# Eight products of the output projection moved between the last head steps of a hybrid decoder layer

## What is computed

```python
a_out = mla_prompt(q_nope, q_rope, c_kv, k_r, w_ukv[l])
b_out = combine_dilations([dilated_prompt(qb, kb, vb, wdw, dl) for wdw, dl in DIL_PATTERNS], xp.dtype)
c_out = conv_module(g_ext, conv_w[l], conv_b[l], conv_ln_g[l], conv_ln_b[l])
xp = xp + jnp.concatenate([a_out, b_out, c_out], axis=-1) @ w_out[l]
hf = rmsnorm(xp, norm_ffn[l])
xp = xp + peer_blocked(hf.reshape(B * T, D), peer_wq[l], peer_subkeys[l], peer_u[l], peer_v[l]).reshape(B, T, D)
```

## Time and profile before

| | us |
|---|---|
| median of 3 runs | 2072.3 (2066.62 to 2073.37) |
| profiled execution, time | 2078.74 |
| profiled execution, span | 2076.9 |
| PE busy | 2055.7 (99%) |
| DVE busy | 1530.8 (74%) |
| ACT busy | 1284.6 (62%) |
| mean granted clock of PE | 0.995 |

### The profile page before, as it was taken

One profiled execution on the slowest core, in us unless ns is written; L12 is line 12 of the kernel. 1 busy time (PEld: TensorE's weight loads), 2 busy tenths in 40 slices (PEclk: granted clock), 3 DMA queues, 4 the chain that ended last, 5 costly groups with the idle time before them and its releaser, 6 DMA issues.

```text
span 2076.9 us, 40622 instructions
## 1 busy us (share of the span) xinstructions
PE 2055.7 (99%) x15546; PEld 1794.8 (86%) x15546; DVE 1530.8 (74%) x3491; ACT 1284.6 (62%) x2535; POOL 119.9 (6%) x138
## 2 busy tenths in 40 slices
PE   8999999999999999999999999999999999999998
PEld 6776799999999888788887758999999998887887
DVE  5844589868899776576678436998688997766766
ACT  5464445658888665565564544556688886555654
POOL 2200010000000010100022000100000001101000
PEclk9999999999999999999999999999999999999999
DMA  9443437776666888898763543577766668888886
GB/s 313 154 150 143 163 126 254 248 253 221 216 215 214 286 304 296 303 319 279 253 226 141 170 170 116 180 253 250 246 221 209 220 214 300 311 290 295 266 269 220
DMA packets 137376, 481.76 MB, mean 232 GB/s; under 512 B 25666, under 2 KB 42082, under 8 KB 130768
## 3 DMA queue, kind: packets, MB, share of 16 engines
q1 hardware_dynamic: 124640, 438.45, 62.6%
q0 software_dynamic: 10496, 40.42, 5.6%
q10 hardware_dynamic: 2048, 0.30, 0.1%
HBM read 475.83 MB, written 104.21 MB: 279 GB/s over the span
## 4 chain that ended last, share of the span: by engine, by line
PE 98%; DVE 1%; ACT 1%; DMA 0%; issue 0%; DVEq 0%; ACTq 0%
PE ps L1194 35%; PE ps L1241 33%; PE ps L827 4%; PE ps L875 4%; PE ps L919 3%; PE ps L1206 3%; PE ps L1157 2%; PE ps L927 2%; PE ps L1165 1%; PE ps L1161 1%; PE ps L884 1%; PE ps L1016 1%; PE ps L1180 1%; PE ps L1019 1%; PE ps L978 1%; PE ps L1032 1%
## 5 line engine op out<-in xcount | busy, mean ns | idle before, releaser
L2165 DVE TENSOR_TENSOR parts<-region,parts 128x1024 fp32r<-128x1024 f32 x512 | 625.6, 1222 | 300.6 <-ACT parts L1509 298.0
L1194 PE MATMUL ps<-tokens_hi,parts 128*128 128x256 f32 x4096 | 760.5, 284 | 0.0
L1509 ACT CAST parts<-region 128x1024 fp32r<-128x1024 f32 x512 | 538.8, 1052 | 271.0 <-PE ps L1241 221.2
L1241 PE MATMUL ps<-parts,parts_hw 128*128 128x512 f32 x3024 | 688.7, 389 | 0.0
L1241 PEld LDWEIGHTS ps<-parts,parts_hw 128*128 128x128 f32 x3024 | 566.8, 188 | 124.0 <-DVE parts_hw L2215 6.9
L1194 PEld LDWEIGHTS ps<-tokens_hi,parts 128*128 128x128 f32 x4096 | 636.6, 188 | 1.0 <-issue 0.8
L1194 PE MATMUL ps<-parts_hw,parts 128*128 128x256 f32 x2048 | 573.7, 280 | 0.0
L1194 PEld LDWEIGHTS ps<-parts_hw,parts 128*128 128x128 f32 x2048 | 386.5, 189 | 0.0
L1555 ACT ACTIVATE big<-ps 128x256 f32<-128x256 f32 (+31 forms) x252 | 131.7, 523 | 146.9 <-PE ps L1194 146.8
L1543 ACT CAST parts_hw<-big 128x256 fp32r<-128x256 f32 x256 | 170.9, 668 | 0.7 <-DVE big L2226 0.7
L1536 ACT ACTIVATE region<-region 128x128 f16<-128x128 f16 x512 | 169.2, 436 | 0.0
(11 more groups left out here) (316 smaller groups left out, 2172.9 us busy)
## 6 DMA issues: line engine op xcount, KB each, us to landing
region<-in_peer_uT SPq DMA_DIRECT2D x256, 512.0 KB, 4.1
region<-in_peer_v SPq DMA_DIRECT2D x256, 512.0 KB, 4.7
out<-in_state_win_k SPq DMA_DIRECT2D x112, 384.0 KB
out<-in_state_win_v SPq DMA_DIRECT2D x112, 384.0 KB
big<-in_window_keysT SPq DMA_DIRECT2D x16, 576.0 KB, 3.8
big<-in_state_win_v SPq DMA_DIRECT2D x48, 192.0 KB, 4.2
region<-in_w_out SPq DMA_DIRECT2D x4, 2048.0 KB, 8.2
big<-in_peer_wq SPq DMA_DIRECT2D x4, 2048.0 KB, 13.7
```

The costliest lines, as they stand in the source:

```text
L1194: mm = pe.matmul(ps[:, j % ZB, 0:SEQ], a, hp[b][:, c, :], start=(c == 0 and n == 0), stop=(c == KD - 1 and n == 2))
L1241: mm = pe.matmul(ps[:, 2 * half + t, :], w_t[a][:, 128 * t:128 * t + 128], v_t[b][:, 512 * half:512 * half + 512], start=(j == 0 and n == ...
L1509: act.copy(hi_t[n % HIGHS], rows_t[n % ROWS]).then_inc(high[l], 1)
L2165: dve.tensor_tensor(lo_t[n % ROWS], rows_t[n % ROWS], hi_t[n % HIGHS], ALU.subtract).then_inc(low[l], 1)
```

## The change

Four of the six "mT" turns, with their copies on ACT, move from behind the loop into step 11, ahead of the window mixes. They hold the heads' outputs of passes 0 to 7. The first two sums, ("xo", 0, 0) and ("xo", 0, 1), are split. Their first four products are made by `begin_out(0)` in step 12 (ahead of owT) and `begin_out(1)` in step 13 (behind olT). The last four are made by `end_out` where the whole sums stood. For that, two jobs "begun" are new, which ACT answers with a nop that moves nothing. The sums stay in their banks meanwhile, so the other jobs from "begun" 0 to "ycT" 1 take turns in the six banks left. From ("xo", 0, 0) on each job has the bank it had.

```diff
         if s == WINDOW_MIX:
+            jobs += [(("mT", g), "A") for g in range(4)]
             jobs += [(("ow", 0), "A"), (("ow", 1), "A")]
         if s == WINDOW_MIX + 1:
-            jobs += [(("owT",), "V"), (("wT",), "V")]
+            jobs += [(("begun", 0), "A"), (("owT",), "V"), (("wT",), "V")]
         if s == WINDOW_MIX + 2:
-            jobs += [(("olT",), "V")]
+            jobs += [(("olT",), "V"), (("begun", 1), "A")]
...
-    jobs += [(("mT", g), "A") for g in range(2 * HP)]
+    jobs += [(("mT", g), "A") for g in range(4, 2 * HP)]
...
-BANK = [LATE.get(name, (n if n < NUM["mT", 0] else n + 6) % 8) for n, (name, _) in enumerate(JOBS)]
+OUT_BANK = (NUM["xo", 0, 0] + 4) % 8
+def bank_of(n, name):
+    if name[0] == "begun":
+        return (OUT_BANK + name[1]) % 8
+    if name in LATE:
+        return LATE[name]
+    if n < NUM["begun", 0]:
+        return n % 8
+    if n >= NUM["xo", 0, 0]:
+        return (n + 4) % 8
+    turn = n - NUM["begun", 0] - 1 - (n > NUM["begun", 1])
+    return (OUT_BANK + 2 + turn % 6) % 8
+BANK = [bank_of(n, name) for n, (name, _) in enumerate(JOBS)]
...
+                def turn_mixed(g):
+                    turn("mT", g, parts=[(oAB[:, t, 128 * g:128 * g + 128], 128, 128, 128 * t) for t in range(2)])
+                def begin_out(t):
+                    wait_moved(pe, "mT", 3)
+                    pe.wait_ge(w_ld[now[0]][5 % 2], 16 * (5 // 2))
+                    o = begin("begun", t)
+                    for k in range(4):
+                        mm = pe.matmul(o[:, 0:512], mixT[:, k, 128 * t:128 * t + 128], wview(5)[:, k, :], start=(k == 0), stop=False,
+                                       skip_group_check=True)
+                    mm.then_inc(product[now[0]], 1)
+                def end_out(t):
+                    o = begin("xo", 0, t)
+                    for k in range(4, KD):
+                        if t == 0 and k == 2 * HP:
+                            wait_moved(pe, "ycT", 1)
+                        mm = pe.matmul(o[:, 0:512], mixT[:, k, 128 * t:128 * t + 128], wview(5)[:, k, :], start=False, stop=(k == KD - 1),
+                                       skip_group_check=True)
+                    mm.then_inc(product[now[0]], 1)
...
                     if s == WINDOW_MIX:
+                        wait_moved(pe, "O", 7)
+                        for g in range(4):
+                            turn_mixed(g)
                         mix_window(0)
                         mix_window(1)
                     if s == WINDOW_MIX + 1:
+                        begin_out(0)
                         wait_moved(pe, "ow", 1)
...
                         mm.then_inc(product[now[0]], 1)
+                        begin_out(1)
                     if s == CONV_STEP[1]:
...
-                        if t < 2:
-                            dense(("xo", c, t), parts, m, 512, conv=(c == 0 and t == 0))
+                        if c == 0 and t < 2:
+                            end_out(t)
+                        elif t < 2:
+                            dense(("xo", c, t), parts, m, 512)
...
                     if s == WINDOW_MIX:
+                        for g in range(4):
+                            copy_mixed(g)
                         for n, dst in enumerate((owS, owS2)):
...
+                    if s in (WINDOW_MIX + 1, WINDOW_MIX + 2):
+                        read("begun", s - WINDOW_MIX - 1)
+                        act.nop().then_inc(moved_a[now[0]], 1)
```

More of the change, by code:

```diff
@@ L865, in keep_busy, with dense @@
                     pe.matmul(o[:, 0:512].rearrange("p (a b) -> p a b", a=4), ident[:, :], iota[:, :].unsqueeze(1).to_broadcast([P, 4, P]), start=True, stop=True)
-            def dense(name, parts, n_out, cols, conv=False, each=None):
+            def dense(name, parts, n_out, cols, each=None):
                 o = begin(*name)
@@ L872, in dense @@
                         wait_moved(pe, each, i)
-                    if conv and i == 2 * HP:
-                        wait_moved(pe, "ycT", 1)
                     mm = pe.matmul(o[0:n_out, 0:cols], lhs, rhs, start=(i == 0), stop=(i == len(parts) - 1))
@@ L1119, in _ @@
                 wait_moved(pe, "O", 2 * NH - 1)
-                for g in range(2 * HP):
-                    turn("mT", g, parts=[(oAB[:, t, 128 * g:128 * g + 128], 128, 128, 128 * t) for t in range(2)])
+                for g in range(4, 2 * HP):
+                    turn_mixed(g)
                 wait_moved(pe, "olT")
@@ L1413, in _, with copy_mixed @@
                     act.copy(va[:, t, :], o[:, 0:384]).then_inc(moved_a[now[0]], 1)
+                def copy_mixed(g):
+                    o = read("mT", g)
+                    act.copy(mixT[:, g, 0:SEQ], o[:, 0:SEQ]).then_inc(moved_a[now[0]], 1)
                 for s in range(2 * NH + 2):
@@ L1473, in _ @@
                         roots(5, slice(9, 12))
-                for g in range(2 * HP):
-                    o = read("mT", g)
-                    act.copy(mixT[:, g, 0:SEQ], o[:, 0:SEQ]).then_inc(moved_a[now[0]], 1)
+                for g in range(4, 2 * HP):
+                    copy_mixed(g)
                 for c in range(2):
```

## The result

The changed kernel takes 2077.3 us in the median (2076.4 to 2080.9), the kernel before 2073.4 (2066.6 to 2075.1) in the runs beside it. The medians are 3.9 us apart. The ratio taken over all executions is 1.0027, 95% interval 1.0015 to 1.0039, which is 5.6 us; it is not that of the medians (1.0019), since the executions of the kernel before scatter over 8 us. So the changed kernel is slower, by less than the 0.3% called "the same" (6.2 us), and its time is just above the range that I gave (2064.5 to 2077). The sign of the forecast was wrong.

What follows compares the result with a forecast made beforehand. TensorE's own queue, busy 99% of the span, was taken as the bound. Layer gains of -2.6 and -1.1 us, plus 1.7 for one clock fall, made -2.0: profiled 2076.7, median 2070.3 us, range 2064.5 to 2077.

Steps and rivals of the forecast that it cites:

- steps 1, 3 and 6: New PE waits in layer 0 before mT 3, begin_out(0) and product 6 of end_out(0): 0.3, 0.6 and 1.1 us.
- steps 1 to 6: Layer 0 at full clock, from the window mixes at 174.55 to the 32nd output-projection record: 205.4 instead of 208.00, -2.6 us.
- rival D: Timed runs don't share the profiled run's two falls, so the change only adds waits: +4.0 us, 2076.3; chance 0.09.
- layer 1's gain: The same stretch in layer 1, ending at 206.57 on layer 0's scale before the change: -1.1 us.
- the same things cost double: At the lower clock, PE's work in the stage takes twice as long: weight loads 0.85 us apart against 0.436 per record.
- I take one fall in the two layers: Clock falls left behind the small products owT to olT: one, costing 1.7 us, bounds 0 and 2 x 1.7.
- The carry to the median: From profiled execution to median of the runs: 2076.7 taken 6.4 us lower, as today's median lies, giving 2070.3.
- C: Slower: clock falls and stays down 10.2 us per layer over dense products, +6.5 us, 2078.8; chance 0.11.
- B: Dense stretches keep the clock up and the waits don't show: -7.7 us, 2064.6; chance 0.12.

Runs made afterwards that it cites:

- e_around: Kernel before plus four useless dense products of 512 columns per layer, two ahead of olT and two behind it: 2075.3 us, ratio 1.0021 to the kernel before.
- e_ahead: Kernel before plus four useless dense products of 512 columns per layer, all ahead of olT: 2079.6 us, ratio 1.0041 to the kernel before.
- e_full: e_both plus mT 3 and ow 0 changing banks, and begin_out(1) cut into two products ahead of olT and two behind: 2067.5 us, ratio 0.9980 to kernel before.
- e_both: Changed kernel with begin_out(0) behind wT, and products 4 and 5 of both sums ahead of the wait for ycT 1: 2069.6 us, 0.9988 of kernel before.
- c1_before: The kernel before, run and profiled again without any edit, on one chip with the changed kernel: 2074.2 us, ratio 1.0005 to the kernel before beside it.

## Why the prediction was wrong
**The waits: right in place and idle time, too small in price.** PE idled 0.31, 0.71 and 1.17 us at the three places where steps 1, 3 and 6 had 0.3, 0.6 and 1.1. But I took the idle time for the price. Taken away one by one they gave 0.25, 0.95 and 1.45 us, 2.65 in all against the 2.0 of the sum. The stage with the clock up is 32.0 where steps 1 to 6 make 31.2 (205.4 less md's start at 174.17), and 29.3 without the waits, which rival D's 203.4 had right: 203.4 - 174.2 = 29.2. Two slips in the sum are too small to matter: 183.65 + 0.6 + 3.49 is 187.74 and not 187.76, and layer 1's gain is 206.57 - 205.4 = 1.2 and not 1.1. And "the same things cost double" holds at the half clock for dense records, not for "os" (0.75 against 0.45) and ycT (1.64 against 1.04). One part of the miss is a row of the wrong clock: "os" takes 0.45 us at the full clock, and I put in 0.75 from a stretch at 0.50. PE came to product 6 earlier, and only waited longer, since that point is set by ACT and DVE. What else a stop costs PE beyond the idle time was not taken apart. The weight load ahead of product 6 shows 2.00 of idle where the matmul shows 1.17.

```profile
200.78 0.30 PEld L1100 LDWEIGHTS ps<-region,big 128*128 128x128 f32 x2 [2.00 <-DVE big L1989]
200.78 5.42 PE L1100 MATMUL ps<-region,big 128*128 128x512 f32 x12 [1.17 <-DVE big L1989]
```

**The clock: the step that failed.** "I take one fall in the two layers", 1.7 us. There were two, of 6.8 and 3.4 us, and they cost 5.1. So both the number of falls and the length of one were too small: in layer 0 dense records follow from 189.22 on, and the clock came back only at 195.1, 5.9 us later, where I had 3 to 4. The prediction itself had named the 4.0 us of small products left between the two begin_out, longer than the stretch ahead of today's fall, and had then put one fall there for no row's sake. The runs show why the moved work doesn't help here. begin_out(0) stands ahead of owT, where the clock had not fallen, and the run of small products behind it stays whole; what keeps the clock up is dense work on both sides of olT (e_around against e_ahead, e_full against e_both). The change trades falls under turns and small products, 17.1 us of half clock in the profile of before, for shorter ones (10.2) and 5.4 us of waits. Measured against executions with the clock up, the median loses as much as before: 2071.9 - 2066.6 = 5.3 before, and 2077.8 - (2066.6 + 5.4) = 5.8 after. The last is an estimate, since none of the changed kernel's 21 executions ran at 0.999.

**The carry to the median.** I moved the profiled time by the 6.4 us between the profile and the median. Of these, 4.5 lie outside the stage in that one execution: its span less the stage in both layers is 2010.8, against 2006.2 in c1_before, 2006.4 in after and 2006.4 in e_full. They were not to be had again, and taking them off was right. The other 1.9 were falls that the median has fewer of: c1_before's profiled execution, with the same 17.1 us of half clock and nothing odd outside the stage, took 2074.1, 1.8 above the 2072.3. I took them off a kernel whose falls I had already counted. The account of the 7.0 us between 2070.3 and 2077.3 is then: waits 2 x 0.7 = 1.4, falls 5.1 - 1.7 = 3.4, carry about 2.

**The rivals.** D (2076.3) came nearest, and that is in part luck. A kernel that doesn't fall pays the waits in full, as D says, but they are 5.4 us and not 4.0, only 8 of 35 executions of the kernel before are of that kind, and the changed kernel does fall. C had the right sign and the right place, falls under dense products, but not its length of 10.2 us. B is what e_full is: no waits, clock up. It gives -4.7 against its neighbours' median, not -7.7. With the page of the Trainium skill that stood beside C ("TensorE: Matmul & The Clock Gate", "A second HAM failure mode: psum-queue depth-cycling"), where short idle times between groups of products make the clock go up and down, the runs agree no better than the trace did: e_ahead has no wait in its stage and falls in nearly all executions, and the changed kernel's three waits end well ahead of the fall or come behind it. To keep the rule against long idle gaps that the Trainium skill gives on the same page ("HAM oscillation — how this bites in real kernels") is not enough here, since PE was busy for 3.40 of the 3.40 us ahead of the fall at 188.30.

What was said of the rest held: the turns' copies on ACT, the nops, the later load of the query weights and the conv_norm behind owT cost nothing that can be seen: e_full, which has all of them, takes 29.4 us for the stage with the clock up, where the kernel before takes 29.3. Behind the stage nothing was lost: the span less the two stages is 2006.4 in after and 2006.2 in c1_before.

## What to carry to other kernels
When work is moved so as to keep TensorE's clock up, look at the whole run of small products and turns, the part behind the fall too, and put dense work into its middle, not at its edge. In this kernel four products ahead of olT left most executions with falls, and with the same four on both sides of it none of twelve ran at 0.997 or less. A sum that is started early shortens the cover of everything its rest waits for: ask for each wait how many records were ahead of it before and how many are after, and do first those parts of all the sums that wait for nothing. Where banks are dealt out anew, read who had each bank last, and who copies it out. And before a change of 0.3% is forecast, ask how the kernel's own executions scatter, and with what.

## What the runs showed of the hardware
- The granted clock fell from 1.00 to 0.50 with PE busy for 3.40 of 3.40 us, behind products of 4 to 64 columns; a median execution of the kernel before loses 5 us to this, one at a mean clock of 0.999 takes 2066.6.
- Four dense products ahead of such a run left 9 of 11 executions at a clock of 0.997 or less, the same four split around its middle none of 12: 2079.6 against 2075.3 us.
- At the half clock dense records took twice as long (0.85 against 0.436 us), "os" 1.7 times (0.75 against 0.45) and the turns ycT 1.6 times (1.64 against 1.04).
- Each stop of PE cost about what it showed as idle or up to 0.3 us more: 0.25 for 0.31, 0.95 for 0.71, 1.45 for 1.17.
